# Gated attention: one score-value product for both directions of a tile, pairs in another order, unread states and levels left out

## The reference

```python
def gla_scan(q, k, v, gk, s0):          # chunks of tokens, decay per key channel
    def step(s, inp):
        qc, kc, vc, gc = inp
        gcum = jnp.cumsum(gc, axis=2)
        rel = jnp.exp(jnp.where(tril[:, :, None], gcum[:, :, :, None] - gcum[:, :, None], -jnp.inf))
        att = jnp.einsum('bhld,bhlsd->bhls', qc, rel * kc[:, :, None])
        o = (jnp.einsum('bhls,bhsv->bhlv', att, vc)
             + jnp.einsum('bhld,bhdv->bhlv', qc * jnp.exp(gcum), s))
        glast = gcum[:, :, -1:]
        s = (jnp.exp(glast[:, :, 0])[..., None] * s
             + jnp.einsum('bhld,bhlv->bhdv', kc * jnp.exp(glast - gcum), vc))
        return s, o

def bidirectional(core, ctx_f, lat_f, ctx_b, lat_b, s0, need_ctx):
    oc_f, sc_f = core(*ctx_f, s0)
    ol_f, _ = core(*lat_f, sc_f)
    oc_b, sc_b = core(*_flip(ctx_b), s0)
    ol_b, _ = core(*_flip(lat_b), sc_b)
    ol = ol_f + jnp.flip(ol_b, axis=1)
    oc = oc_f + jnp.flip(oc_b, axis=1) if need_ctx else None
    return oc, ol
```

## Time and profile before

| what | us |
|---|---|
| median of three runs | 2076.28 |
| lowest and highest | 2074.93, 2077.32 |
| profiled execution, own time | 2075.65 |
| span of its instructions | 2073.9 |

### The profile page before, as it was taken

The page is one execution under the profiler, slowest core; times in us unless marked ns, Lnnn a source line. Parts: engine busy times, 40 slices in busy tenths (PEclk is TensorE's granted clock), DMA queues, the critical chain, the costliest instruction groups (busy, mean ns, idle before and its releaser), DMA issues.

```text
span 2073.9 us, 28996 instructions
## 1 busy us (share of the span) xinstructions
PE 1987.8 (96%) x12190; PEld 1213.0 (58%) x12190; DVE 724.4 (35%) x1504; ACT 571.2 (28%) x1240; POOL 93.2 (4%) x94
## 2 busy tenths in 40 slices
PE   6999999999999999999999999998999997999997
PEld 2444777785654444444444474444775665888886
DVE  2541775006760010000000065555758777010001
ACT  4111325415551030000000051224355687120000
POOL 0000330000000000000000000001211110000000
PEclk9999999999999999999999999999999998999999
DMA  6433111233201122222112131211224110334442
GB/s 276 162 147 124 41 41 43 100 123 123 84 17 66 71 72 71 81 81 81 62 70 76 61 122 63 79 61 62 83 93 175 63 49 16 122 132 153 152 145 89
DMA packets 27999, 193.50 MB, mean 93 GB/s; under 512 B 3004, under 2 KB 4285, under 8 KB 5854
## 3 DMA queue, kind: packets, MB, share of 16 engines
q1 hardware_dynamic: 27826, 191.51, 25.4%
q10 hardware_dynamic: 44, 0.14, 0.0%
HBM read 190.59 MB, written 1.05 MB: 92 GB/s over the span
## 4 chain that ended last, share of the span: by engine, by line
PE 87%; DVE 6%; ACT 4%; issue 2%; DMA 1%; SPq 0%; POOL 0%; ACTq 0%; DVEq 0%; POOLq 0%
PE psum L707 86%; DVE ws_sb L2005 1%; ACT ws_sb L1523 1%; ACT arena_sb L1523 1%; DVE gl_tmp_sb L2005 1%; DVE ws_sb L2008 1%; ACT L1523 1%; ACT wide_sb L1523 1%; DMA arena_sb<-w 1%; DVE arena_sb L2014 0%; PE psum L1117 0%; DVE arena_sb L2005 0%; PE psum L966 0%; ACT hT_sb L1523 0%; DVE hT_sb L2008 0%
## 5 line engine op out<-in xcount | busy, mean ns | idle before, releaser
L707 PE MATMUL psum<-hT_sb,ring_sb 128*128 128x512 f32 (+2 forms) x2272 | 797.9, 512 | 1.9 <-ACT hT_sb L1523 1.9
L707 PEld LDWEIGHTS psum<-hT_sb,ring_sb 128*128 128x128 f32 (+1 forms) x2272 | 427.9, 189 | 364.1 <-issue 339.5
L707 PE MATMUL psum<-arena_sb,ring_sb 128*128 128x512 f32 (+1 forms) x1216 | 396.2, 487 | 5.0 <-DVE small_sb L2011 1.9
L707 PEld LDWEIGHTS psum<-arena_sb,ring_sb 128*128 128x128 f32 x1216 | 231.5, 191 | 167.0 <-issue 144.0
L1523 ACT ACTIVATE ws_sb<-psum 128x512 f32<-128x512 f32 (+4 forms) x256 | 132.8, 525 | 695.7 <-PE psum L707 674.5
L707 PE MATMUL psum<-ring_sb,hT_sb 128*128 128x256 f32 (+3 forms) x1248 | 240.8, 372 | 0.8 <-ACT hT_sb L1523 0.5
L707 PEld LDWEIGHTS psum<-ring_sb,hT_sb 128*128 128x128 f32 (+1 forms) x1248 | 194.1, 176 | 53.5 <-issue 22.0
L2005 DVE TENSOR_TENSOR arena_sb<-ws_sb,psum 128x512 f32<-128x512 f32 (+1 forms) x44 | 24.4, 554 | 414.7 <-PE psum L707 414.7
L2008 DVE SCALAR_TENSOR_TENSOR xT_sb<-psum,mod_sb,xT_sb 128x256 f32<-128x256 f32 x48 | 23.2, 484 | 387.2 <-PE psum L707 386.7
L1523 ACT ACTIVATE wide_sb<-xT_sb 128x512 f32<-128x512 f32 (+1 forms) x40 | 21.8, 545 | 392.1 <-PE psum L707 295.0
L2008 DVE SCALAR_TENSOR_TENSOR ws_sb<-ws_sb,cols_sb 128x512 f32<-128x512 f32 (+1 forms) x176 | 123.8, 703 | 6.3
(11 more groups left out here) (172 smaller groups left out, 1474.9 us busy)
## 6 DMA issues: line engine op xcount, KB each, us to landing
ring_sb<-w SPq DMA_DIRECT2D x146, 1024.0 KB, 4.8
hT_sb<-w SPq DMA_DIRECT2D x16, 1024.0 KB, 4.8
arena_sb<-w SPq DMA_DIRECT2D x8, 1024.0 KB, 17.0
ring_sb<-w SPq DMA_DIRECT2D x8, 768.0 KB, 4.1
xT_sb<-x SPq DMA_DIRECT2D x1, 2048.0 KB, 8.1
const_sb<-consts SPq DMA_DIRECT2D x1, 2048.0 KB, 9.3
y<-xT_sb SPq DMA_DIRECT2D x1, 1024.0 KB, 4.8
ring_sb<-w SPq DMA_DIRECT2D x2, 256.0 KB, 3.8
```

Source lines behind the costliest of these rows:

```text
L707: return nc.tensor.matmul(o, l, r, start=start, stop=stop)
```

## The change

- `pair_at`: pairs run over directions first, then steps, then pairs of heads: p % 2 is the direction, p // 2 % 4 the step k, p // 8 the pair of heads. Pairs 4m and 4m + 1 are the first visits of two tiles and pairs 4m + 2 and 4m + 3 the second visits of the same two tiles, from the other side.
- The near parts of a tile's first visit (k even) are masked and reduced into a seventh part of that tile's own `near_tile`; at the second visit the reduce covers all seven. The far parts of both visits lie in one half of PSUM bank 1, chosen by the tile. `far_copy` and `near_copies` run only at the second visit, and so does the product of scores and values.
- At k = 0 there is no output at all and no exponentials or products for the state's queries; at k = 3 none for the next state.
- `st_gla` has a place per direction instead of per head. k = 1 and 2 copy the output into `o0`, k = 3 adds to it. `square_sums` follow two pairs behind, at pairs with k = 0 and 2.
- The counts in the waits on `gla_far`, `gla_att`, `gla_kdec` and `gla_out` follow `tiles_done` and `states_done`.

Of the context lines only those are kept that say in which function and loop a line stands.

```diff
--- before.py
+++ after.py
@@ -413,12 +413,13 @@
-        st_gla = area(ws, 7424, GLA_H, GLA_DV)
+        st_gla = area(ws, 7424, 2, 2, GLA_DV)
-        near = wide[:, 0, 0:2 * NEAR * 32]
-        near_sum = wide[:, 1, 0:64].rearrange("p (h c) -> p h c", h=2)
+        wide_flat = wide.rearrange("p a b -> p (a b)")
+        near_tile = [wide_flat[:, 448 * i:448 * i + 448].rearrange("p (h c) -> p h c", h=2) for i in range(2)]
+        near_sum = wide_flat[:, 896:960].rearrange("p (h c) -> p h c", h=2)
@@ -489,8 +490,16 @@
         def pair_at(p):
-            d, k, h = p // 8, p // 2 % 4, p % 2 * 2
+            d, k, h = p % 2, p // 2 % 4, p // 8 * 2
+
+        def tiles_done(p):
+
+            return p // 4 * 2 + max(p % 4 - 2, 0)
+
+        def states_done(p):
+
+            return p // 8 * 6 + min(p % 8, 6)
         def level_bank(u):
@@ -1162,8 +1171,9 @@
-                    mm(psum[:, level_bank(u), 0:2 * P], beyond[d], gk[:, j, d, h * P:(h + 2) * P])
-                    for hh in range(2):
+                    if k < 3:
+                        last = mm(psum[:, level_bank(u), 0:2 * P], beyond[d], gk[:, j, d, h * P:(h + 2) * P])
+                    for hh in range(2 if k > 0 else 0):
@@ -1173,7 +1183,7 @@
-                        pe.wait_ge(S["gla_far"], p)
+                        pe.wait_ge(S["gla_far"], tiles_done(p))
                     for hh in range(2):
                         for b in range(NEAR):
@@ -1184,7 +1194,7 @@
-                        far = 256 * d + P * hh
+                        far = 256 * (j % 2) + P * hh
@@ -1195,17 +1205,20 @@
                 def outputs(p):
-                    pe.wait_ge(S["gla_att"], p + 1)
+                    n = tiles_done(p)
+                    if k % 2 == 1:
+                        pe.wait_ge(S["gla_att"], n + 1)
-                    for hh in range(2):
+                    for hh in range(2 if k > 0 else 0):
-                        mm(o, att0[:, p % 2, hh], v0[:, j, h * GLA_DV:(h + 1) * GLA_DV], stop=(k == 0))
-                        if k > 0:
-                            mm(o, qk[p % 3][:, LEV, hh], st_gla[:, h], start=False)
-                    pe.wait_ge(S["gla_kdec"], p + 1)
-                    for hh in range(2):
+                        if k % 2 == 1:
+                            mm(o, att0[:, n % 2, hh], v0[:, j, h * GLA_DV:(h + 1) * GLA_DV], stop=False)
+                        last = mm(o, qk[p % 3][:, LEV, hh], st_gla[:, d, hh], start=(k == 2))
+                    if k < 3:
+                        pe.wait_ge(S["gla_kdec"], states_done(p) + 1)
+                    for hh in range(2 if k < 3 else 0):
@@ -1709,6 +1722,7 @@
                 def level_exp(p, i):
+                    k = pair_at(p)[1]
@@ -1718,41 +1732,46 @@
-                        f(kdec0[:, p % 3], psum[:, level_bank(u), 0:2 * P], ACT.Exp, scale=1.0 / GLA_NORM)
-                        ins = f(qk[p % 3][:, LEV].rearrange("p a b -> p (a b)"), psum[:, level_bank(u), 2 * P:4 * P], ACT.Exp, scale=1.0 / GLA_NORM)
+                        if k < 3:
+                            ins = f(kdec0[:, p % 3], psum[:, level_bank(u), 0:2 * P], ACT.Exp, scale=1.0 / GLA_NORM)
+                        if k > 0:
+                            ins = f(qk[p % 3][:, LEV].rearrange("p a b -> p (a b)"), psum[:, level_bank(u), 2 * P:4 * P], ACT.Exp, scale=1.0 / GLA_NORM)
                 def far_copy(p):
-                    d = p // 8
+                    n, j = tiles_done(p), pair_at(p)[3]
-                    if p >= 2:
-                        act.wait_ge(S["gla_out"], p - 1)
-                    own(f(att0[:, p % 2].rearrange("p a b -> p (a b)"), psum[:, 1, 256 * d:256 * d + 256], ACT.Copy).then_inc(S["gla_far"], 1), S["gla_far"])
+                    if n >= 2:
+                        act.wait_ge(S["gla_out"], p - 3)
+                    own(f(att0[:, n % 2].rearrange("p a b -> p (a b)"), psum[:, 1, 256 * (j % 2):256 * (j % 2) + 256], ACT.Copy).then_inc(S["gla_far"], 1), S["gla_far"])
                 def near_copies(p):
-                    act.wait_ge(S["gla_near"], p + 1)
+                    n = tiles_done(p)
+                    act.wait_ge(S["gla_near"], n + 1)
-                        ins = f(att0[at, p % 2, :, at], near_sum[at], ACT.Copy)
+                        ins = f(att0[at, n % 2, :, at], near_sum[at], ACT.Copy)
                 for p in range(2):
                 for p in range(16):
-                    far_copy(p)
+                    if p % 4 >= 2:
+                        far_copy(p)
-                    near_copies(p)
+                    if p % 4 >= 2:
+                        near_copies(p)
-                    if p >= 10:
+                    if p >= 4 and p % 4 < 2:
                 for p in (14, 15):
@@ -2224,25 +2243,28 @@
-                        tt(o, o, src, ALU.mult)
-                    dve.wait_ge(S["gla_exp"], LEVEL_UNITS * (p + 1))
-                    link(copy(tile_decay[:, p % 3], e[:, LEV, :, (P - 1, 0)[d]]))
-                    own(tt(e[:, LEV], e[:, LEV], q0[:, j, h0:h0 + 2], ALU.mult).then_inc(S["gla_qk"], 1), S["gla_qk"])
+                        ins = tt(o, o, src, ALU.mult)
+                    if k > 0:
+                        dve.wait_ge(S["gla_exp"], LEVEL_UNITS * (p + 1))
+                        if k < 3:
+                            link(copy(tile_decay[:, p % 3], e[:, LEV, :, (P - 1, 0)[d]]))
+                        ins = tt(e[:, LEV], e[:, LEV], q0[:, j, h0:h0 + 2], ALU.mult)
+                    own(ins.then_inc(S["gla_qk"], 1), S["gla_qk"])
                 def taken(p):
-                    if d == 0:
+                    if k in (1, 2):
-                    else:
-                        tt(o, o, psum[:, 2, :], ALU.add)
+                    elif k == 3:
+                        ins = tt(o, o, psum[:, 2, :], ALU.add)
-                        ins = copy(st_gla[:, h0:h0 + 2], psum[:, 3, :].rearrange("p (a b) -> p a b", a=2))
-                    else:
+                        ins = copy(st_gla[:, d], psum[:, 3, :].rearrange("p (a b) -> p a b", a=2))
+                    elif k < 3:
                         for hh in range(2):
-                            ins = stt(st_gla[:, h0 + hh], st_gla[:, h0 + hh], tile_decay[:, p % 3, hh:hh + 1],
+                            ins = stt(st_gla[:, d, hh], st_gla[:, d, hh], tile_decay[:, p % 3, hh:hh + 1],
@@ -2250,14 +2272,19 @@
-                    own(tt(near.rearrange("p (h c) -> p h c", h=2), psum[:, 0, 0:2 * NEAR * 32].rearrange("p (h c) -> p h c", h=2),
+                    near, n = near_tile[j % 2], tiles_done(p)
+                    own(tt(near[:, :, 0:NEAR * 32], psum[:, 0, 0:2 * NEAR * 32].rearrange("p (h c) -> p h c", h=2),
-                    if p > 0:
-                        dve.wait_ge(S["gla_att"], p)
-                    own(V.tensor_reduce(near_sum, near.rearrange("p (h l c) -> p h c l", h=2, c=32), AX_X, ALU.add).then_inc(S["gla_near"], 1), S["gla_near"])
-                    kd = kdec0[:, p % 3]
-                    dve.wait_ge(S["gla_exp"], LEVEL_UNITS * (p + 1))
-                    own(tt(kd, kd, k_tok0[:, j, h0 * P:(h0 + 2) * P], ALU.mult).then_inc(S["gla_kdec"], 1), S["gla_kdec"])
+                    if k % 2 == 0:
+                        V.tensor_reduce(near[:, :, NEAR * 32:], near[:, :, 0:NEAR * 32].rearrange("p h (l c) -> p h c l", c=32), AX_X, ALU.add)
+                    else:
+                        if n > 0:
+                            dve.wait_ge(S["gla_att"], n)
+                        own(V.tensor_reduce(near_sum, near.rearrange("p h (l c) -> p h c l", c=32), AX_X, ALU.add).then_inc(S["gla_near"], 1), S["gla_near"])
+                    if k < 3:
+                        kd = kdec0[:, p % 3]
+                        dve.wait_ge(S["gla_exp"], LEVEL_UNITS * (p + 1))
+                        own(tt(kd, kd, k_tok0[:, j, h0 * P:(h0 + 2) * P], ALU.mult).then_inc(S["gla_kdec"], 1), S["gla_kdec"])
```

## The result

Before, the median is 2076.47 us (2074.93 to 2077.32, 4 runs); after, 2064.05 us (2062.08 to 2065.70, 4 runs). The ratio is 0.9937, 95% interval 0.9924 to 0.9951: 12.4 us or 0.6% faster. Forecast were 15.4 us off and 2060.9 us; the range of 2056.5 to 2065.5 holds the result, near its upper end.

A forecast was written before the change was run, and what follows sets the result against it. PE's instructions were taken to bound the GLA stage; outputs 10.2, tile_levels 4.3, start-up 0.5 and tail 0.4 gave 15.4 us off 2075.65, so 2060.3, or 2060.9 us as median. Range 2056.5 to 2065.5 us.

The forecast's parts named there:

- the clock is under 1.00 after 480 us: GLA stage: sign that would show the prediction wrong, PE's granted clock below full after that time.
- a late clock: Start of the GLA stage: clock rising later than before; a late rise or one more dip costs 3 us.
- a dip: Later stages: one half-clock dip more or fewer, 3 us either way, allowed for in the range.
- Outputs, 10.2 us: PE's output products in the GLA stage: 24 products of 0.425 us fewer, 41.1 to 30.9 us.
- tile_levels, 4.3 us: PE's level products at k=3 and k=0: eight parts of 0.53 us saved; lower bound 3.4 us at 0.43 each.
- Tail, 0.4 us: PE's waits for DVE in the last two pairs: 1.4 us saved, 1.0 lost, net between 0 and 1.
- Start-up at half clock, 0.5 us: First tile_levels: the cut pair of products costs about 1.06 instead of 0.53 us, so 0.5 us more saved.
- -1 to +3 us: Start-up of the GLA stage: open allowance for whether the clock rises as early as before.
- The clock rival: GLA or later stages: PE's short waits drop the clock to half and the kernel ends slower, 2106 us; chance 0.02.
- gaps of 1.7 us left the clock at 1.00: Tail before the change, 593 to 605 us: clock held through waits of 1.73 and 1.64 us; argued against a clock drop.
- The DVE/ACT loop: GLA pairs: DVE/ACT floor 7.0 us at k odd, just under PE; as rival bound, 2065.8 us, chance 0.09.
- the table of passes: Second eight pairs, per iteration: PE 51.1 us in sum beside DVE/ACT 50.6 us.

The follow-up runs named there:

- fill_start: Changed kernel plus idle PE products in the waits at the start of the GLA stage; stage 120.52 us, median 2057.46 us, ratio to before 0.9913.
- before_fill: Kernel before plus the idle products of fill_start; stage 134.71 us, median 2076.03 us, ratio to before 0.9991.
- the repetitions: Changed kernel profiled twice more, unaltered; stage 123.76 us each, median 2062.55 us in the one with a median.
- fill_tail: Changed kernel plus idle PE products only at the end of the GLA stage; stage 122.12 us, median 2063.01 us, ratio to before 0.9933.
- part kernels: The change in two parts, each with idle products at the stage's start: cuts_fill (stage 126.42 us) and collect_fill (128.85 us).
- collect_fill: Changed kernel with all levels and states computed as before, plus idle products at the stage's start; stage 128.85 us, ratio to before 0.9964.
- cuts_fill: Kernel before with only unread states and levels left out, plus idle products at the stage's start; stage 126.42 us, ratio to before 0.9938.
- exp_preload: Changed kernel with one early exponential on ACT, so its table loads while ACT is idle; stage 120.16 us, ratio to before 0.9925.
- preload_fill: Changed kernel with the early exponential and smaller idle products at the stage's start; stage 119.20 us, median 2057.25 us, ratio to before 0.9912.
- reduce_twice_fill: Changed kernel with idle products at the stage's start and the reduce of k-odd pairs done twice; stage 124.38 us, ratio to before 0.9934.
- the first repetition: Changed kernel run again unaltered, first of two times; stage 123.76 us, median 2062.55 us, ratio to before 0.9934.

## Why the prediction was right, and what was off

The mechanism was right, and so was the largest term: PE's instructions set the stage. The clock was not: "the clock is under 1.00 after 480 us" is one of the signs that the prediction named for being wrong, and it came, at the start until 482.3 us and again in the tail. The stage lasted 125.5 and 123.8 us instead of the 121.6 forecast; the range held the result because it left room for a late clock and for a dip. Two comparisons take the clock out. With full clock on both sides (fill_start against before_fill) the change is worth 14.2 us; the terms without the half clock one are 10.2 + 4.3 + 0.4 = 14.9. With the same 6.8 us of half clock at the start on both sides (the repetitions) it is 137.04 - 123.76 = 13.3 us, and 1.6 more without the half clock at the end, by fill_tail: 14.9, beside the prediction's whole sum of 15.4.

- **Outputs, 10.2 us: right.** 48 instructions fewer (176 to 128 of 128x256), six products 2.79 us. The part kernels bear it out: collect_fill, without 16 of the 24 products and with all levels, is 6.48 us shorter in the middle, 6.8 less the new wait; the other eight are among the 4.33 us of cuts_fill's middle and the 3.5 of its tail.
- **tile_levels, 4.3 us: too much by 0.8.** The prediction took 0.53 per part and gave 0.43 as the lower bound; measured are 0.44 us, 3.5 in all. (In the start-up at full clock the two half parts give only 0.45 us together.) What is left of a part takes 0.63 or 0.64 instead of 0.54, so it keeps the entry gap. The lower bound was the value to take.
- **Tail, 0.4 us: too little by 0.4, the clock aside.** The two last waits fell to 0.94 and 0.85 as forecast (1.0). Before the last scores PE waits 0.57 and before outputs(14) 0.72, where 0.8 each was expected. 3.1 us of waits in all instead of 3.9: 0.8 us saved.
- **Start-up at half clock, 0.5 us: the term that failed.** The prediction said the cut products there cost double and are saved double, and left "-1 to +3 us" open for the moment at which the clock rises. In the first profile it rose 3.4 us of half clock later than before, and the start-up gained nothing: 11.64 instead of 11.39 us. In the repetitions it rose after the same 6.8 us (10.21 and 10.22 us to the first scores, 1.2 less than before). In fill_start, at full clock, the start-up gains 0.45 us over before_fill, not the 0.9 of its two level parts; part of it only lengthens a wait for ACT.
- **The clock rival, in small: it came true.** The prediction gave it 0.02, for a loss of more than the whole gain; that didn't come. But all three profiles of the changed kernel have 3.4 us of half clock at the end, neither of the two of the kernel before has any. It costs 1.6 us, and the longer half clock at the start 1.7 us where it occurs: 14.9 becomes 13.3 or 11.6 us, the lengths seen. The median's 12.4 lies between, but it also holds what the rest of the kernel did. The prediction had argued that gaps of 1.7 us left the clock at 1.00; here it fell with gaps of 0.57 and 0.72 us before it. The rule in the Trainium skill, "TensorE: Matmul & The Clock Gate", section "HAM oscillation — how this bites in real kernels", names a long idle gap as what drops the clock. The trace doesn't bear it out in the tail: it has the drop, but not a gap longer than those that before did no harm. Why it falls in the tail of the changed kernel and not of others with the same waits (fill_start, exp_preload, preload_fill) stays open; reduce_twice_fill, whose tail falls too, has a longer wait there (1.71 us).
- **The DVE/ACT loop: right that it is just under PE.** 6.98 us between weighs where 7.0 was worked out, and no wait of PE between the second scores and the last. Doubling the reduce showed its room: 2.2 us lost for 3.8 us of work in the second eight pairs, nothing for as much in the first eight. One slip stands in the table of passes: PE's last two are given 6.1 us, though from p = 14 on PE makes no levels, as the prediction's own paragraph on the tail has it at 3.7. So PE's sum is 46.3 us and not 51.1, under the 50.6 of DVE and ACT; over the first six passes it is 38.9 against 37.4, and there PE leads. Scores start 6.63, 5.80, 5.77, 7.53, 7.06 and 6.23 us apart for the first six, as the table gives them, then 4.30, of which 0.57 is the wait. The forecast time is not touched, since the waits were costed in the tail.

## What to carry to other kernels

When the chain of waits shows one engine without a break for a whole stage, count the instructions a change takes from that engine, price each by the difference between starts of the parts around it, and check the next engine's loop per iteration, not its share of busy time: here DVE and ACT are 80% and 54% busy in the long window and their loop is within a few microseconds of the bound. If you leave out a part of a group, take the price without its entry gap. Where a stage starts with a chain of short works and waits, look at the granted clock before counting gains there: idle products in the waits and an early table load brought the stage from 123.8 to 119.2 us (4.6 us, of which 1.6 is the stretch at the end, whose cause is open), beside 13.3 us for the change itself.

## What was not expected of the hardware

- The same program spends 6.8 us at half clock at the start of the stage in some executions and 10.2 us in others. The 3.4 us more lengthened the stage by 1.7 us. 6.8 us of half clock cost the kernel before 2.3 us and the changed one 1.6, since part of it lies in a wait (1.3 and 1.97 us) and since at full clock PE waits for ACT instead.
- On the kernel before, the same fillers brought the clock to 1.00 and the stage down by 2.3 us, but the median by only 1.8 us with an interval that reaches equality (0.9982 to 1.0001). The part of the kernel behind the stage also has stretches at half clock, 40 to 60 us in all by execution, and moves by up to 5 us: from 1465.6 us (44 us at half clock, fill_start) to 1470.4 (61 us, the first repetition).
